# When a fused two-block transformer kernel loads its Sqrt and Exp tables, and in which order VectorE finishes a projection

## The reference, cut to what matters

```python
# block 1, each of 2 layers (D_MODEL 1024, D_FF 2816)
h = x * (1.0 + sc1) + sh1
y = mixer(h)                                       # q, k, v; attention; @ w_o
x = layer_norm(DEEPNORM_ALPHA * x + (1.0 + g1) * y, ln_g[l, 0], ln_b[l, 0])
h = x * (1.0 + sc2) + sh2
y = swiglu(h, w_ffn_in[l], w_ffn_out[l])
x = layer_norm(DEEPNORM_ALPHA * x + (1.0 + g2) * y, ln_g[l, 1], ln_b[l, 1])
# block 2, each of 2 layers, on x and on a second stream of 256 context tokens
x = x + 0.5 * gate * (swiglu(modulate(rms_norm(x, g))))   # up, down
x = x + gate * (attention(modulate(rms_norm(x, g))) @ w_out)
x = x + 0.5 * gate * (swiglu(modulate(rms_norm(x, g))))
```

## Time and profile before

| | |
|---|---|
| three runs | 2691.02, 2697.57, 2698.38 us; median 2697.57 |
| span of the profiled execution | 2697.4 us |
| time around that span | none is recorded for it; span and median differ by 0.2 us |
| PE busy | 2552.8 us (95%) |
| DVE busy | 1747.1 us (65%) |
| ACT busy | 1084.1 us (40%) |
| mean granted TensorE clock | 0.986 |
| DMA | 413.88 MB, mean 153 GB/s |

### The profile page before, as it was taken

How to read it: one execution, slowest core, us unless ns; L and a number is a source line. 1 busy time by engine, 2 the same in 40 slices (tenths; PEclk the granted TensorE clock), 3 DMA queues, 4 the chain that set the end, 5 groups by cost and what they waited for, 6 DMA issues and landing times.

```text
span 2697.4 us, 41940 instructions
## 1 busy us (share of the span) xinstructions
PE 2552.8 (95%) x16532; PEld 2184.0 (81%) x16532; DVE 1747.1 (65%) x3313; ACT 1084.1 (40%) x2104; POOL 136.6 (5%) x92
## 2 busy tenths in 40 slices
PE   4879999899999999999998999999999999998999
PEld 3858998879998888888766788888788888777999
DVE  7677776667776677545678856554665544577754
ACT  2445545445444333223356333322333323345553
POOL 1000100000100111000000011100011100000010
PEclk9989999999999999999999999999999999999999
DMA  8936875925663454444510354434344443513653
GB/s 284 274 107 199 273 244 173 283 79 196 198 216 110 141 171 157 133 135 113 165 47 1 126 164 139 150 118 132 110 141 141 138 131 107 153 63 121 209 178 120
DMA packets 354894, 413.88 MB, mean 153 GB/s; under 512 B 24753, under 2 KB 291930, under 8 KB 354634
## 3 DMA queue, kind: packets, MB, share of 16 engines
q1 hardware_dynamic: 352496, 404.13, 46.7%
q0 software_dynamic: 1120, 5.70, 0.6%
q10 hardware_dynamic: 1082, 1.38, 0.2%
HBM read 409.56 MB, written 5.27 MB: 154 GB/s over the span
## 4 chain that ended last, share of the span: by engine, by line
PE 81%; DVE 10%; DMA 4%; ACT 3%; issue 1%; SPq 0%; ACTq 0%; DVEq 0%
PE bank L898 79%; DVE ada_partial L1617 3%; DVE weight_lo L692 2%; PE bank L1201 2%; DMA raw_weights<-in_w_in_ab_dram 2%; DMA raw_weights<-in_w_in_cd_dram 1%; ACT weight_hi L1288 1%; DMA raw_weights<-in_w_ffn_in_dram 1%; ACT H_hi L1385 0%; DVE bank L1931 0%; ACT tmp L1348 0%; ACT X L1392 0%; DVE rstd L1878 0%; DVE X L1838 0%; DMA raw_weights<-in_w_out_dram 0%
## 5 line engine op out<-in xcount | busy, mean ns | idle before, releaser
L692 DVE TENSOR_TENSOR weight_lo<-raw_weights,weight_hi 128x512 fp32r<-128x512 f32 x1024 | 771.7, 761 | 806.4 <-ACT weight_hi L1288 793.0
L1288 ACT ACTIVATE weight_hi<-raw_weights 128x512 fp32r<-128x512 f32 x1024 | 633.6, 629 | 1254.3 <-PE bank L898 1151.2
L898 PE MATMUL bank<-H_hi,weight_hi 128*128 128x256 f32 (+1 forms) x2832 | 957.2, 338 | 31.4 <-DVE weight_lo L692 20.4
L898 PE MATMUL bank<-H_lo,weight_hi 128*128 128x256 f32 (+1 forms) x2832 | 941.9, 333 | 0.0
L898 PE MATMUL bank<-H_hi,weight_lo 128*128 128x256 f32 (+1 forms) x2832 | 940.9, 332 | 0.0
L898 PEld LDWEIGHTS bank<-H_hi,weight_hi 128*128 128x128 f32 x2832 | 543.3, 192 | 114.8 <-issue 53.6
L898 PEld LDWEIGHTS bank<-H_hi,weight_lo 128*128 128x128 f32 x2832 | 543.6, 192 | 50.3
L898 PEld LDWEIGHTS bank<-H_lo,weight_hi 128*128 128x128 f32 x2832 | 543.9, 192 | 47.5 <-issue 0.5
L1617 DVE SCALAR_TENSOR_TENSOR ada_partial<-raw_weights,silu_c,ada_partial 128x512 f32<-128x512 f32 x616 | 442.1, 745 | 1.3 <-DVE ada_partial L1617 0.2
L898 PE MATMUL bank<-hidden_hi,weight_hi 128*128 128x256 f32 (+1 forms) x1056 | 357.8, 339 | 4.3 <-DVE weight_lo L692 4.2
L898 PE MATMUL bank<-hidden_lo,weight_hi 128*128 128x256 f32 (+1 forms) x1056 | 355.5, 337 | 0.0
(11 more groups left out here) (189 smaller groups left out, 1855.8 us busy)
## 6 DMA issues: line engine op xcount, KB each, us to landing
raw_weights<-in_w_ada_dram SPq DMA_DIRECT2D x120, 1024.0 KB, 5.7
raw_weights<-in_w_ffn_up_dram SPq DMA_DIRECT2D x88, 1024.0 KB, 5.3
raw_weights<-in_w_ffn_in_dram SPq DMA_DIRECT2D x44, 1024.0 KB, 6.6
raw_weights<-in_w_ffn_down_dram SPq DMA_DIRECT2D x32, 1024.0 KB, 5.2
raw_weights<-in_w_in_dram SPq DMA_DIRECT2D x18, 1024.0 KB, 5.6
raw_weights<-in_w_ffn_out_dram SPq DMA_DIRECT2D x16, 1024.0 KB, 7.5
raw_weights<-in_w_in_ab_dram SPq DMA_DIRECT2D x12, 1024.0 KB, 9.5
raw_weights<-in_w_in_cd_dram SPq DMA_DIRECT2D x12, 1024.0 KB, 8.5
```

Source lines behind the costliest of these rows:

```text
L692: eng.tensor_tensor(WL[:, p.g % SPLIT, 0:p.kt * CW].rearrange("p (t n) -> p t n", n=CW), raw_ap(ch.n, ch.kt, CW)[:, p.k0:p.k0 + p.kt, :], ...
L898: return pe.matmul(o, w, x, start=start, stop=stop, skip_group_check=True)
L1288: act.activation(WH[:, p.g % SPLIT, 0:p.kt * CW].rearrange("p (t n) -> p t n", n=CW), raw_ap(ch.n, ch.kt, CW)[:, p.k0:p.k0 + p.kt, :], ACT ...
```

## The change

What it does, part by part:

- In every projection ScalarE runs one Sqrt on a constant (`root_unread`) after group 0, and in every qkv stage one Exp (`exp_unread`) after the last splits and ahead of the last copy out of PSUM. Nothing reads either; the compiler's table loads move to them.
- In the last group of a projection, VectorE makes the rest of the weights for all pieces but the last, updates X, tells that tile 6 is ready (`x_tile6`), finishes tile 7, and only then makes the rest of the last piece. The hosted `w_ada` product is spread over one piece fewer.
- In block 1, X is multiplied by ALPHA ahead of the wait for TensorE, and each tile is then updated from PSUM in one instruction, as in block 2.
- TensorE (mean, and squares of rms) and ScalarE (squares of rms) wait for tile 6 and for tile 7 apart.
- Squares go to four buffers in place of two.
- The unread matmuls are fewer: in an ln stage 21 in place of 36, in an rms stage 23 in place of 34.

The diff, cut to its core:

```diff
@@ before.py 1108, TensorE @@
                 if s.kind == "ln":
                     if done:
                         pe.wait_ge(ev_dve.sem, done)
+                    elif t == 6:
+                        pe.wait_ge(x_tile.sem, s.tile6)
+                    elif t == 7:
+                        pe.wait_ge(x_ready.sem, s.x)
                     ins = mm(B_STAT[:, 0:s.n], ones[:, :], X[:, t, 0:s.n], t == 0, t == NT - 1)
...
-                mm(bank[:, 0:s.n], ones[:, :], T1[:, t % 2, 0:s.n], t == 0, t == NT - 1).then_inc(stat_mm.sem, 1)
+                mm(bank[:, 0:s.n], ones[:, :], SQUARES[t % 4][:, 0:s.n], t == 0, t == NT - 1).then_inc(stat_mm.sem, 1)
...
         def stats(s, before):
 
-            busy(6 if s.kind == "rms" else 4)
-            pe.wait_ge(x_ready.sem, s.x)
+            busy(4 if s.kind == "rms" else 3)
+            if before.kind != "proj":
+                pe.wait_ge(x_ready.sem, s.x)
             for m in range(3 if before.kind == "proj" else 0, 4):
                 sums(s, m)
             if s.kind == "ln":
                 busy(4)
                 for t in range(NT):
                     squares(s, t, B_T[0])
-                    busy(1)
             if s.last_ln:
                 context()
             if s.kind == "rms":
-                busy(10)
+                busy(6)
                 spread_rstd(s)
-                busy(18)
+                busy(13)
             else:
-                busy(20)
+                busy(14)
@@ before.py 1344, ScalarE @@
         def square(s, t):
-            act.wait_ge(stat_mm.sem, s.stat + t - 1)
-            act.activation(T1[:, t % 2, 0:s.n], X[:, t, 0:s.n], ACT.Square).then_inc(stat_in.sem, 1)
+            act.wait_ge(stat_mm.sem, s.stat + t - 3)
+            act.activation(SQUARES[t % 4][:, 0:s.n], X[:, t, 0:s.n], ACT.Square).then_inc(stat_in.sem, 1)
...
         def stats(s, before):
+            early = s.kind == "rms" and before.kind == "proj"
+            if early:
+                act.wait_ge(x_tile.sem, s.tile6)
+                square(s, 6)
             act.wait_ge(x_ready.sem, s.x)
-            for t in range(6 if s.kind == "rms" and before.kind == "proj" else 0, NT):
+            for t in range(7 if early else 0, NT):
...
+                if it is s.items[-1]:
+                    act.activation(EXP1[:, :], ZERO[:, 0:1], ACT.Exp)
                 used(one, lambda _: it.chunk.pieces[-1])
                 pair, kind, n = PAIR[it.grp.n % 2], it.what[0], it.n
...
         def proj(s, norm):
             for m, g in enumerate(s.groups):
+                if m == 1:
+                    act.activation(ROOT1[:, :], EPS[:, 0:1], ACT.Sqrt)
@@ before.py 1815, VectorE, proj @@
             for m, g in enumerate(s.groups):
+                last = g is s.groups[-1]
                 for ch in g.chunks:
-                    ahead_of(one, lambda _: ch, (lambda _: g.host) if g.host and ch is g.chunks[-1] else None)
-                used(one, lambda _: g.chunks[-1].pieces[-1])
-                pair = PAIR[g.grp.n % 2]
+                    if last and ch is g.chunks[-1]:
+                        n_ahead = len(ch.pieces) - 1
+                        for i, p in enumerate(ch.pieces[:-1]):
+                            ahead(one, lambda _: p, split, late)
+                            if g.host:
+                                ada(one, lambda _: g.host, i, n_ahead)
+                    else:
+                        ahead_of(one, lambda _: ch, (lambda _: g.host) if g.host and ch is g.chunks[-1] else None)
...
                 if s.first:
-                    for j in range(2):
-                        t = 2 * m + j
-                        ins = dve.tensor_scalar(T2[:, j, 0:n], pair[j][:, 0:n], ad[:, 8 * s.gate + t, :], None, ALU.mult)
-                    chain.link(ins)
-                    ins = dve.scalar_tensor_tensor(out=X[:, 2 * m:2 * m + 2, 0:n], in0=X[:, 2 * m:2 * m + 2, 0:n],
-                                                   scalar=ALPHA, in1=T2[:, :, 0:n], op0=ALU.mult, op1=ALU.add)
-                else:
...
+                    x = X[:, 2 * m:2 * m + 2, 0:n]
+                    chain.link(dve.tensor_scalar(x, x, ALPHA, None, ALU.mult))
+                used(one, lambda _: g.chunks[-1].pieces[-1])
+                pair = PAIR[g.grp.n % 2]
+                for j in range(2):
+                    t = 2 * m + j
+                    for v in range(n // T):
+                        cols = slice(v * T, v * T + T)
+                        gate = GS[:, t, v:v + 1] if s.half else ad[:, 8 * s.gate + t, v:v + 1]
+                        ins = dve.scalar_tensor_tensor(out=X[:, t, cols], in0=pair[j][:, cols], scalar=gate,
+                                                       in1=X[:, t, cols], op0=ALU.mult, op1=ALU.add)
+                    if last and j == 0:
+                        ins.then_inc(x_tile.sem, 1)
                 chain.link(ins)
                 dve.sem_inc(g.grp.tally.sem, 1)
             dve.sem_inc(x_ready.sem, 1)
+            ahead(one, lambda _: s.groups[-1].chunks[-1].pieces[-1], split, late)
```

More of the change, by code:

```diff
@@ L201, in __init__ @@
                  shift=None, silu=None, sink=None, sq=None, steps=None, take=None, unroll=None, vblk=None,
-                 vcol=None, vrow=None, vw=None, what=None, x=None, x_out=None, a32=None, halves=None, sub=None):
+                 vcol=None, vrow=None, vw=None, what=None, x=None, x_out=None, a32=None, halves=None, sub=None,
+                 tile6=None):
         self.kind, self.ada, self.bias, self.bias_in = kind, ada, bias, bias_in
@@ L305, in _build @@
     RI = sb("row_scale", [P, 4])
+    ROOT1, EXP1 = sb("root_unread", [P, 1]), sb("exp_unread", [P, 1])
     base = (nc.sbuf_base + 63) // 64 * 64
@@ L490, in add @@
         now = dict(h_wait=h_ready.total, o_wait=o_done.total, x=x_ready.total,
-                   bias_in=bias_in.total, last_ln=False)
+                   bias_in=bias_in.total, last_ln=False, tile6=x_tile.total)
         PLAN.append(Stage(kind, **{**now, **k}))
@@ L539, in ffn @@
             first=first,
-            ready=act_ready.total, x_out=x_ready.take(1),
+            ready=act_ready.total, x_out=x_ready.take(1), tile6=x_tile.take(1),
             need=need(ada, gate))
@@ L548, in w_out @@
         add("proj", hosted=all_hosted, n=n, groups=groups, ada=ada, gate=gate, half=False, hidden=False, first=first,
-            ready=o_done.total, x_out=x_ready.take(1),
+            ready=o_done.total, x_out=x_ready.take(1), tile6=x_tile.take(1),
             need=need(ada, gate))
```

14 lines of the change are left out of this document (4 added, 10 removed).

## The result

The changed kernel took 2664.53 us in the median of four runs (2660.99 to 2669.68), the kernel before 2697.98 beside it: a ratio of 0.9878, 95% interval 0.9861 to 0.9896. The forecast was 2671 and the range 2663 to 2682. The profiled execution has a span of 2659.1 us, 38.3 less than that of before; since it is the shortest of the four, the medians' 33.4 is the better size of the gain.

The account below looks back on a forecast made before the run. TensorE's waits hold 81% of the span, so gains must lie where TensorE waits. Terms 7.7 + 2.7 + 1.6 + 0.4 + 7.4 + 6.2 + 0.5 = 26.5 us; 2697.6 - 26.6 = 2671 us, range 2663 to 2682.

Parts of the forecast that it names:

- X right behind TensorE: RMS norms behind block 2's feed-forward parts: X starts behind TensorE's last product, 1.25 us for the rest of the split.
- wide RMS norm behind a feed-forward part: Block 2, three norms: root at 1238.63 in place of 1241.21, gain 2.58 us each, 7.7 in all.
- the attention output: Block 2, RMS norm at 1520: X starts 1.37 us earlier; with the squares and the load, gain 2.7 us.
- layer norms behind feed-forward parts: Block 1, two norms: centring 1.6 us earlier, centring to root 2.1 us shorter; 3.7 each, 7.4 in all.
- the other two: Layer norms behind block 1's attention outputs: 1.0 us ahead of the centring, 2.1 behind; 3.1 each, 6.2 in all.
- rival C: Start of attention, three places: the new Exp load is hidden, 3 x 1.1 us better, 2667 us; chance 6%.
- Fewer unread matmuls: 0: Norms: issuing fewer unread matmuls itself gains 0 us, while the clock stays up.
- of which I take 0.4: RMS norm right behind block 1: squares start when they did; only the load's exposed part goes, 0.4 us.
- Exp: 0.2 each: Start of attention, three times: scores start 1.05 us later, Exp no longer waits 1.28; 0.2 each, 0.5 in all.
- Rival D: Roots keep a load of their own because the set changes again before them: 9 x 0.76 = 7, 2678 us; chance 3%.
- Rival B: Stages behind norms: fewer unread matmuls drop TensorE to 1.2 GHz, 12.8 us a stage; slower, 2735 with five; chance 4%.
- Rival A: Norms: the shortened chains meet a second one and half the gain is given back, 2684 us; chance 14%.

Follow-up runs that it names:

- no_root_load: The changed kernel without the unread Sqrt in the projections, so the table loads stand at the roots again: 2670.47 us, ratio 0.9900 to the kernel before.
- no_exp_load: The changed kernel without the unread Exp ahead of v's copies, its load behind the first row minimum again: 2664.38 us, ratio 0.9874 to before.

## Why the prediction was right

The sign, the range and nearly every step held: the order of events, X right behind TensorE, at the roots 2.61 us per wide RMS norm behind a feed-forward part (2.58), 2.68 at the attention output (2.7), 3.8 and 3.4 in the layer norms behind feed-forward parts (3.7), 3.0 and 2.7 in the other two (3.1), 0.76 for the load in a wide RMS norm, nothing for the loads in the projections, no gain to speak of from Exp. The gain was 33.4 us and not 26.6 (the prediction's terms add up to 26.5). The time, 2664.5, lies outside the forecast's own 2667 to 2675 and inside the stated range only because that was stretched down to 2663 for rival C, a hidden Exp load, which did not come: that part is luck. These terms were mis-sized:

- "Fewer unread matmuls: 0". In the last layer's norm 36 unread rows ran from the spread to the first product (4.29 us from 2493.76), which started at 2497.80, while H_lo had been ready since 2496.03. With 26 rows the product comes 3.3 us behind the spread and not 4.4. This is 1.1 of the 1.5 us missing there; the rows stand below, before first. The old counts in the changed kernel show the same price, and 5.1 us for it over the nine norms. In a wide norm behind a projection it moved the first product by 0.4, which the chain of H tiles took back.
- "of which I take 0.4" for the norm behind block 1. It had no load to lose: the layer norm just before had loaded Sqrt, and its row says nine loads for ten roots. It gained 2.3 us by two other ways: root to root 14.61 us before and 13.89 after, with four buffers (15.07 in the version with two), and root to product 7.23 against 5.60 us. There ten unread matmuls, partly at half clock, had held the spread to 862.81 us, while the reciprocal had ended at 861.47.
- "Exp: 0.2 each". With the full clock it was right: Exp at 5.71 us against 5.96 in no_root_load, 0.25 earlier. In the profiled execution of the change half clock fell into the scores and cost more than was won. The longer wait isn't shown to be its cause: half clock came with waits of 2.1 to 2.3 us as well, and stayed away in an execution with 3.27. no_exp_load gives about 0 in sum.
- The rest, from 30 us in the norms to 33.4, stays open. The clock may be part of it: in the one execution of before with two unused tiles it fell inside three more norms, 1.6 us each. How often it does in before and how rarely in the change was not counted, and 3 us is the scatter of the medians.

Put back one at a time, the parts cost the nine norms 9.5 us (VectorE's order), 8.0 (two buffers), 5.3 (unread matmuls between the sums), 5.1 (the old counts around them) and 4.1 (the loads at the roots). They overlap, so they don't add up. ALPHA * X ahead of the wait, and the separate waits for tiles 6 and 7, were not put back alone. Rival D, a load left at every root, was priced at 9 x 0.76; it would have cost 4.1, as the layer norms hide their load behind the sums.

The last norm in the timelines of before and after (spread, unread rows, first H_lo, first product):

```profile
2493.38 0.45 PE L898 MATMUL bank<-rstd,ones 1*128 1x64 f32 x8
...
2493.76 4.29 PE L898 MATMUL bank<-ones,ident 128*128 128x128 f32 x36
...
2495.55 0.48 DVE L1766 SCALAR_TENSOR_TENSOR H_lo<-tmp,ada,H_hi 128x256 fp32r<-128x256 f32 x1 [0.24 <-ACT H_hi L1383]
...
2497.80 0.36 PE L898 MATMUL bank<-H_hi,weight_hi 128*128 128x256 f32 x1
```

```profile
2457.32 0.45 PE L901 MATMUL bank<-rstd,ones 1*128 1x64 f32 x8
...
2457.70 3.17 PE L901 MATMUL bank<-ones,ident 128*128 128x128 f32 x26
...
2459.49 0.48 DVE L1781 SCALAR_TENSOR_TENSOR H_lo<-tmp,ada,H_hi 128x256 fp32r<-128x256 f32 x1 [0.24 <-ACT H_hi L1394]
...
2460.63 0.36 PE L901 MATMUL bank<-H_hi,weight_hi 128*128 128x256 f32 x1
```

Rival B (the clock without fillers) was not what this change met, and the kernel without unread matmuls gives its size: 1.2 to 1.7 us per wide RMS norm. Behind a wide projection the low clock lasted 10.2 us, about half of it ahead of the first product, and never a stage. The Trainium skill's rule in "TensorE: Matmul & The Clock Gate" (HAM oscillation), that idle gaps bring back half clock, is borne out by those 164 us. The 15 and 11 fewer unread matmuls of the change brought no such loss: 64 and 88 us at half clock, 77 before. The drain that the Trainium skill adds to a load ("ScalarE: Activation LUTs", What ACT_TABLE_LOAD costs) is nowhere: 0.02 us between load and root in no_root_load, and 4.1 us for all loads together where the page would give some 15 (an estimate). Rival A names what the old counts would have done in the shortened chains, but not its size: they cost 5.1 us of the norms' 30, a sixth and not half.

## What to carry to other kernels

Work that only fills time in an in-order queue has to be cut along with the wait it covers: each wait shortened makes the filler the next thing that is late, while none at all lets the clock fall. When one engine's piece of preparation stands ahead of the result others wait for, change places first; then ask what now stands between that result and its next use, as the rest did ahead of the centring. And compare stages by an instruction that both kernels issue the same number of times: it separated 0.7 us effects that medians with 3 us of scatter could not.

## What the runs showed of the hardware

- Moving the region that holds the two hidden tiles by 64 bytes in a partition changed the pace of matmuls that read them: 12 products of 128x512 in 2.747 against 2.720 us, 12 of 128x256 in 1.36 to 1.413 against 1.440. In the three runs with the region at byte 139136 and the eleven with it at 139200 the wide pace went with the place each time. Why is open; to put them at one place for the wide stages and at the other for the narrow ones wasn't tried.
- ALPHA * X in place, 128x512 from SBUF to SBUF with a constant, took 0.42 us, where the difference of two tiles of the same size (VectorE's rest of a split) takes 0.69.
- With a table load directly before it, the root starts 1.32 us behind the end of the activation before: 0.02, the load's 1.28, and 0.02. What the load costs is less where the function waits for something else meanwhile: 0.76 us here, as the last sum takes 0.55.
